# Expert weights in transfers of 4 MB with 32 KB runs, and the column order of W1 that goes with them

## What is computed

```python
for e in range(32):
    gu = tok @ w1[e] + b1[e]                       # w1[e]: 1024 x 2048
    gate = min(gu[:, :1024], 7); lin = clip(gu[:, 1024:], -7, 7)
    act = (lin + 1) * gate * sigmoid(1.702 * gate)
    out += combine[:, e:e+1] * (act @ w2[e] + b2[e])   # w2[e]: 1024 x 1024
```

## Time and profile before

| | |
|---|---|
| times of three executions | 1139.09, 1140.57, 1141.27 us |
| the profiled execution | 1139.39 us, its span 1137.7 us |
| PE busy | 1083.0 us (95%), 4926 matmul instructions |
| DVE, ACT busy | 195.9 us (17%), 139.7 us (12%) |
| DMA | 432.94 MB in 41954 packets, 381 GB/s over the span |
| large loads of expert weights | 191 of 2 MB, 42.1 us from issue to landing (median) |
| granted TensorE clock | 1.00 |

### The profile page before, as it was taken

The page is one execution under the profiler, slowest core; times in us unless marked ns, Lnnn a source line. Parts: engine busy times, 40 slices in busy tenths (PEclk is TensorE's granted clock), DMA queues, the critical chain, the costliest instruction groups (busy, mean ns, idle before and its releaser), DMA issues.

```text
span 1137.7 us, 11181 instructions
## 1 busy us (share of the span) xinstructions
PE 1083.0 (95%) x4926; PEld 423.5 (37%) x4926; DVE 195.9 (17%) x499; ACT 139.7 (12%) x285; POOL 14.9 (1%) x34
## 2 busy tenths in 40 slices
PE   7999999999999999999999989999999999999996
PEld 5474544733333333333333333333323333333332
DVE  1630011311211111111111111111111111111111
ACT  2114111201100001010000000000000000000001
POOL 0004000000000000000000000000000000000000
PEclk9999999999999999999999999999999999999999
DMA  9824526699999999999999999999999999999995
GB/s 346 322 105 148 220 75 262 273 424 429 427 429 425 429 427 428 427 428 429 426 429 427 428 427 429 427 427 428 427 428 429 427 428 427 429 426 429 427 428 217
DMA packets 41954, 432.94 MB, mean 381 GB/s; under 512 B 4252, under 2 KB 5808, under 8 KB 17328
## 3 DMA queue, kind: packets, MB, share of 16 engines
q1 hardware_dynamic: 40272, 431.26, 90.6%
q10 hardware_dynamic: 1632, 0.95, 0.3%
HBM read 431.14 MB, written 1.05 MB: 380 GB/s over the span
## 4 chain that ended last, share of the span: by engine, by line
PE 64%; DMA 35%; DVE 1%; ACT 0%; issue 0%; DVEq 0%; ACTq 0%
DMA ring<-in_expert_w_dram 34%; PE bank L314 23%; PE bank L329 11%; PE bank L956 9%; PE bank L338 4%; PE bank L1112 2%; PE bank L1092 2%; PE bank L304 2%; PE bank L275 2%; PE bank L320 1%; PE bank L1017 1%; PE bank L291 1%; PE bank L296 1%; PE bank L946 1%; PE bank L1039 0%; PE bank L284 0%
## 5 line engine op out<-in xcount | busy, mean ns | idle before, releaser
L314 PE MATMUL bank<-ring,work 128*64 128x512 f32 x2048 | 450.5, 595 | 19.0 <-DMA ring<-in_expert_w_dram 19.0
L314 PEld LDWEIGHTS bank<-ring,work 128*64 128x64 f32 x2048 | 142.3, 137 | 324.9 <-issue 280.2
L329 PE MATMUL bank<-ring,work 128*64 128x512 f32 x1024 | 229.5, 594 | 19.5 <-DMA ring<-in_expert_w_dram 19.0
L329 PEld LDWEIGHTS bank<-ring,work 128*64 128x64 f32 x1024 | 72.2, 137 | 170.9 <-issue 135.2
L870 DVE TENSOR_SCALAR work<-bank 128x512 f32<-128x512 f32 x32 | 22.1, 692 | 480.0 <-PE bank L314 480.0
L956 PE MATMUL bank<-ring 128*128 128x512 f32 x224 | 98.5, 594 | 0.0
L650 ACT ACTIVATE work<-work 128x512 f32<-128x512 f32 x32 | 20.2, 630 | 515.8 <-DVE work L870 515.8
L338 PE MATMUL bank<-work,putT 64*128 64x512 f32 x256 | 63.6, 615 | 0.8 <-ACT work L670 0.8
L360 DVE TENSOR_TENSOR work<-bank,vecs 128x512 f32<-128x512 f32 x32 | 22.1, 692 | 228.3 <-PE bank L291 227.2
L956 PEld LDWEIGHTS bank<-ring 128*128 128x128 f32 x224 | 41.8, 190 | 48.4 <-issue 48.2
L275 PE MATMUL bank<-xn,pick 128*64 128x512 f32 x248 | 58.6, 593 | 0.0
(11 more groups left out here) (179 smaller groups left out, 443.5 us busy)
## 6 DMA issues: line engine op xcount, KB each, us to landing
ring<-in_expert_w_dram SPq DMA_DIRECT2D x191, 2048.0 KB, 42.1
ring<-in_w_in_dram SPq DMA_DIRECT2D x8, 2048.0 KB, 19.7
ring<-in_w_out_dram SPq DMA_DIRECT2D x2, 2048.0 KB, 7.8
ring<-in_w_branch_attn_dram SPq DMA_DIRECT2D x1, 2048.0 KB, 8.2
ring<-in_w_branch_pool_dram SPq DMA_DIRECT2D x1, 2048.0 KB, 7.6
ring<-in_w_in_dram SPq DMA_DIRECT2D x1, 1296.0 KB, 7.8
xs<-in_x_dram SPq DMA_DIRECT2D x2, 512.0 KB, 4.2
ring<-in_expert_w_dram SPq DMA_DIRECT2D x1, 1024.0 KB, 42.8
```

The lines of the kernel that those rows point to most:

```text
L314: mm = pe.matmul(dst, hTe[:, at:at + SLOTS], w[:, col:col + BANK], start=(k == 0 and not bias_first), stop=(k == KD - 1 and bias_first), s ...
L329: mm = pe.matmul(ps_out[SLOTS * half:SLOTS * (half + 1), :], actT_e[:, at:at + SLOTS], w[:, col:col + BANK], start=(k == 0), stop=(k == KD ...
```

## The change

The ring becomes 5 places of 4 MB. An expert's W1 is two transfers and its W2 one, and a partition holds 4 rows of W1 or 8 of W2: one run of 32 KB. While blocks and scratch still share the ring, and for the refill of expert 2's W1, the seven first chunks (`IN_HALVES`) go in halves of 2 MB, each with a semaphore of its own, in the same order of waits as before; blocks lie in halves of three places. W2's last transfer goes in four pieces.

With 8 rows of W2 in a partition, hidden columns 8g to 8g+7 belong to partition g. PE gets that order by the way it reads W1: `quarter` takes four columns, skips four, and so on; quarter 0 is the first four of each eight, quarter 1 the others. The bias is read in the same way from rows twice as wide, of which both quarters hold a copy. `down` then uses the same transposes with step 4. Reading the gathered rows and the first picks, `every` has step 4 instead of 2; the router's transposes (L1118) and its weights are in plain order, for which a second copy of the gain (`V_GR`) is transposed: eight tiny transposes at L996 instead of two.

```diff
-    RING = 10
-    CHUNK_N = 4096
+    RING = 5
+    CHUNK_N = 8192
+    HALF_N = CHUNK_N // 2
-    SLOT_ORDER = (1, 9, 2, 3, 4, 6, 7, 8, 5, 0)
+    SLOT_ORDER = (0, 1, 3, 4, 2)
+    IN_HALVES = RING + W1_CHUNKS
...
-            base = S0 * CHUNK_N + slot * 2048 + at
+            base = S0 * HALF_N + (0, 1, 5, 6, 7, 2, 3, 4)[slot] * 2048 + at
...
-        TAIL = ((0, 2), (2, 3), (3, 4))
+        TAIL = ((0, 4), (4, 6), (6, 7), (7, 8))
...
-            return ring[:, i % POSITIONS, :]
+            at = (i - 1) % POSITIONS
+            return ring[:, at // 2, at % 2 * HALF_N:(at % 2 + 1) * HALF_N]
...
+        def quarter(ap, q):
+            at = q // 2 * FE
+            return ap[:, at:at + FE].rearrange("p (g h i) -> p h g i", h=2, i=4)[:, q % 2]
...
-                mm = pe.matmul(dst, bias_pick[rows, :], b1_rows[rows, :], start=first, stop=not first, skip_group_check=True)
+                mm = pe.matmul(dst, bias_pick[rows, :], quarter(b1_rows[rows, :], q % 2), start=first, stop=not first,
+                               skip_group_check=True)
...
-                    col = a * 2 * FE + q * BANK
-                    mm = pe.matmul(dst, hTe[:, at:at + SLOTS], w[:, col:col + BANK],
+                    mm = pe.matmul(dst, hTe[:, at:at + SLOTS], quarter(w[:, a * 2 * FE:(a + 1) * 2 * FE], q),
...
             used(B_G0 + 2)
-            load_w1(0, 0)
+            w1_half(0, 0, 0)
             sp.wait_ge(s["attn_ps"], TT)
-            load_w1(0, 1)
+            w1_half(1, 0, 1)
             used(B_G0 + 3)
-            load_w1(0, 2)
+            w1_half(0, 0, 1)
             used(B_WP)
-            load_w1(0, 3)
-            for c in (0, 1):
-                load_w1(1, c)
+            w1_half(0, 1, 0)
+            w1_half(0, 1, 1)
+            w1_half(1, 0, 0)
             sp.wait_ge(s["mergedT_ps"], 2 * TT)
-            for c in (2, 3):
-                load_w1(1, c)
+            w1_half(1, 1, 0)
+            w1_half(1, 1, 1)
             used(B_WO)
-            for c in range(W2_CHUNKS):
-                load_w2(0, c)
+            for h in range(2):
+                load_half(w2_chunk(0, 0), h, w2_dram(0, 0))
+            for c in range(W1_CHUNKS):
+                for h in range(2):
+                    if (c, h) != (W1_CHUNKS - 1, 1):
+                        sp.wait_ge(half_used, 2 * c + h + 1)
+                    else:
+                        sp.wait_ge(gemm1, 1)
+                    w1_half(2, c, h)
...
-                    sp.wait_ge(chunk_used, n + 1 - sum(last < n for last in W1_LAST + W2_LAST))
+                    sp.wait_ge(half_used, 3 * W1_FIRST.index(n) + 2)
 
             for e in range(1, E):
-                if e < E - 1:
+                if 1 < e < E - 1:
                     for c in range(W1_CHUNKS):
                         slot_free(w1_chunk(e + 1, c) - RING)
-                        load_w1(e + 1, c)
-                for c in range(W2_CHUNKS):
-                    slot_free(w2_chunk(e, c) - RING)
-                    if (e, c) != (E - 1, W2_CHUNKS - 1):
-                        load_w2(e, c)
-                        continue
-                    n, src = w2_chunk(e, c), w2_dram(e, c)
+                        load(w1_chunk(e + 1, c), w1_dram(e + 1, c))
+                n, src = w2_chunk(e, 0), w2_dram(e, 0)
+                slot_free(n - RING)
+                if e < E - 1:
+                    load(n, src)
+                else:
                     for i, (a, b) in enumerate(TAIL):
...
-                mm = pe.transpose(bank[4][:, at:at + W1_CHUNKS], every(g2_rows, W1_ROWS, a), ident[0:W1_CHUNKS, 0:W1_CHUNKS])
+                pe.transpose(bank[4][:, at:at + W1_CHUNKS], every(g2_rows, W1_ROWS, a), ident[0:W1_CHUNKS, 0:W1_CHUNKS])
+                at += KD
+                mm = pe.transpose(bank[4][:, at:at + W1_CHUNKS], g2_rows[:, a * P:(a + 1) * P], ident[0:W1_CHUNKS, 0:W1_CHUNKS])
...
-                    mm = pe.transpose(ps[:, j * P:(j + 1) * P], every(xs[:, tt, :], W1_ROWS, k), ident[:, :])
+                    mm = pe.transpose(ps[:, j * P:(j + 1) * P], xs[:, tt, k * P:(k + 1) * P], ident[:, :])
...
-                    pe.wait_ge(*chunk_landed(n))
-                    mm = up(pe, chunk_slot(n), c)
-                    if c < W1_CHUNKS - 1:
-                        mm.then_inc(chunk_used, 1)
+                    if n >= IN_HALVES:
+                        pe.wait_ge(*chunk_landed(n))
+                    for h in range(2):
+                        if n < IN_HALVES:
+                            pe.wait_ge(*half_landed(n, h))
+                        mm = up(pe, chunk_slot(n), c, range(2 * h, 2 * h + 2))
+                        if (c, h) != (W1_CHUNKS - 1, 1):
+                            mm.then_inc(half_used, 1)
                 mm.then_inc(gemm1, 1)
...
                 n = w2_chunk(E - 1, 0)
-                pe.wait_ge(*chunk_landed(n))
-                down(pe, chunk_slot(n), 0)
-                scatter(pe).then_inc(scattered, 1)
-                n = w2_chunk(E - 1, 1)
                 for i, (a, b) in enumerate(TAIL):
                     pe.wait_ge(tail_in[i], 16)
-                    mm = down(pe, chunk_slot(n), 1, range(a, b))
+                    mm = down(pe, chunk_slot(n), 0, range(a, b))
+                    if i == 0:
+                        scatter(pe).then_inc(scattered, 1)
```

More of the change, by code:

```diff
@@ L91, in scratch @@
         def scratch(slot, at, size):
-            flat = ring[:, :, :].rearrange("p s n -> p (s n)")
-            base = S0 * CHUNK_N + slot * 2048 + at
-            return flat[:, base:base + size]
+            base = S0 * HALF_N + (0, 1, 5, 6, 7, 2, 3, 4)[slot] * 2048 + at
+            return ring[:, :, :].rearrange("p s n -> p (s n)")[:, base:base + size]
         hT = scratch(0, 0, KD * T).rearrange("p (k t) -> p k t", k=KD)
@@ L142, in block_kernel @@
         vec_rows = putT[0:10, 0:P]
[L143 to L144 removed]
+        vecs = sb("vecs", [P, 34])
+        V_G1, V_PB, V_PS, V_QK, V_G2, V_GR = 0, 8, 12, 16, 18, 26
         pool_wsb = sb("pool_wsb", [P, G, P])
@@ L176, in block_kernel @@
         chunk_in = [sem(f"chunk_in{i}") for i in range(RING)]
-        TAIL = ((0, 2), (2, 3), (3, 4))
+        half_in = [[sem(f"half_in{i}_{h}") for h in range(2)] for i in range(RING)]
+        TAIL = ((0, 4), (4, 6), (6, 7), (7, 8))
         tail_in = [sem(f"tail_in{i}") for i in range(len(TAIL))]
-        chunk_used = sem("chunk_used")
+        half_used = sem("half_used")
         names = """gain_in consts inv_ok ident_ok vec_row_ok vec_ps vec_ok x_rms x_norm xT_ps hT_dve hT_act
@@ L244, in w2_chunk @@
             return (e + 1) * (W1_CHUNKS + W2_CHUNKS) + (W1_CHUNKS - W2_CHUNKS if e < E - 1 else -W2_CHUNKS) + c
+        W1_FIRST = [w1_chunk(e, 0) for e in range(E)]
         W1_LAST = [w1_chunk(e, W1_CHUNKS - 1) for e in range(E)]
@@ L252, in chunk_landed, with half_landed @@
         def chunk_landed(n):
-            return chunk_in[n % RING], 16 * (n // RING + 1)
+            return chunk_in[n % RING], 16 * (n // RING - (IN_HALVES - 1 - n % RING) // RING)
+        def half_landed(n, h):
+            return half_in[n % RING][h], 16 * (n // RING + 1)
         def w1_dram(e, c):
@@ L303, in up_bias, with up @@
                 rows = slice(E * q, E * (q + 1))
-                mm = pe.matmul(dst, bias_pick[rows, :], b1_rows[rows, :], start=first, stop=not first, skip_group_check=True)
-            return mm
-        def up(pe, w, c, bias_first=True):
-            for a in range(W1_ROWS):
+                mm = pe.matmul(dst, bias_pick[rows, :], quarter(b1_rows[rows, :], q % 2), start=first, stop=not first,
+                               skip_group_check=True)
+            return mm
+        def up(pe, w, c, rows=range(W1_ROWS), bias_first=True):
+            for a in rows:
                 k = c * W1_ROWS + a
@@ L319, in transpose_act @@
             for j in range(4):
-                mm = pe.transpose(ps_gate[:, j * P:(j + 1) * P], every(act_e, W2_ROWS, j), ident[:, :])
+                mm = pe.transpose(ps_gate[:, j * P:(j + 1) * P], every(act_e, 4, j), ident[:, :])
             return mm
@@ L395, in load_block, with load, load_half, w1_half @@
                 sp.dma_start(dst, src.rearrange("(k p) n -> p k n", p=P)).then_inc(block_in[i], 16)
[L397 to L403, removed]
+            def load(n, src):
+                sp.dma_start(chunk_slot(n), src).then_inc(chunk_in[n % RING], 16)
+            def load_half(n, h, src):
+                cols = slice(h * HALF_N, (h + 1) * HALF_N)
+                sp.dma_start(chunk_slot(n)[:, cols], src[:, cols]).then_inc(half_in[n % RING][h], 16)
+            def w1_half(e, c, h):
+                load_half(w1_chunk(e, c), h, w1_dram(e, c))
             for i in range(N_BLOCKS):
@@ L527, in _ @@
                               src.rearrange("a (h d) -> a h d", h=1).to_broadcast([1, 2, HD])).then_inc(s["vec_row_ok"], 16)
```

(15 more changed lines are left out.)

10 lines of the change are left out of this document (5 added, 5 removed).

## The result

The median after is 1150.01 us (six executions, 1148.12 to 1153.11) beside 1140.63 us for the kernel before (six, 1139.09 to 1141.27). The ratio is 1.0080, with an interval of [1.0067, 1.0094]: slower by 9.4 us, where 0.2 us less was forecast. The profiled execution took 1149.25 us, its span is 1147.5 us, 9.8 us above that of before. These 9.8 us are what has to be found.

What follows compares the result with a forecast made beforehand. The prediction took the DMA stream of expert weights, with its start and PE tail, as the bound. Terms -6.3 + 3.4 + 2.2 + 0.5 = -0.2 us gave 1140.4 us beside the median of 1140.57; range 1136.2 to 1147.0.

Steps and rivals of the forecast that it cites:

- PE before the stream: PE work ahead of the weight stream: more gain transposes, plain router transposes, step four in L284 free; together +0.5 us.
- The rule on lines of 16 bytes: SBUF accesses within one 16-byte line run at full rate, each new line costs something; L314's four-column read would be free.
- Longer runs: Expert weight DMA: 88 whole transfers with 32 KB runs take 0.73% less time, -6.3 us, bounds nothing to 8 us saved.
- the straight line through 2 KB and 16 KB: DMA run cost from two measured run sizes: 0.03687 ns a byte and 9.0 ns a run.
- half a semaphore write a run: DMA packets: half a semaphore write for each run, eight runs to a transfer, counted within the 9.0 ns a run.
- Both rivals with less saving: Expert weight DMA: no saving from 32 KB runs, 1146.7 us, chance 0.08; half the saving, 1143.6 us, chance 0.10.
- a lower DMA rate: Rival: 128 weight runs starting 32 KB apart slow DMA; 1155 us at one per cent, chance 0.05.
- The gap: DMA waits at the first whole transfer, expert 1's W2, near 248 us: +2.2 us, bounds 1.0 and 3.2.
- The tail: At the end, 32 instead of 16 L329 instructions stand after expert 30's W2 lands: +3.4 us.
- PE's reading of W1: L314's moving operand takes four columns, skips four: no cost, with 2.3 us of cover an expert.
- The rival with PE as the bound: L314 stretches by over a sixth, so PE sets the pace; at double some 1530 us, chance 0.05.
- The laggards lag less: Rival: slow DMA engines trail less in the tail, half of 7 us, 3.5 us: 1136.9 us, chance 0.13.

Runs made afterwards that it cites:

- the split transfers: The changed kernel with normed rows written in PE's reading order, each whole 4 MB transfer issued as two of 2 MB with 16 KB runs: 1147.89 us.
- the experiment: The kernel before with L314's moving operand reading every fourth column of W1: 1575.11 us.

## Why the prediction was wrong

*The step that failed* is one clause in "PE before the stream": "L284 takes every fourth element instead of every second; L320 (fourth) and L291 (second) load 209 ns each: nothing." The rows were read rightly and did not carry over. L320 and L291 are transposes, whose loads take 209 ns with either step, and do so after the change too: L303, the old L291, now with step four, 211 ns. L284's loads took 196 ns with step two and 329 with step four, and 16 of its instructions 3.73 us instead of 1.99. I priced the line from another kind of instruction, though the trace had L284 itself, whose 196 ns say nothing of step four. No row showed that case, and the forecast gave this edit one value and no bounds. The rule on lines of 16 bytes was quoted for the moving operand of L314 and not tried on L284, which with step four takes one f32 from each line.

*What it measured.* The late start of 9.65 us instead of 0.5 is 0.30 from before 211 us (forecast 0.5), 1.75 for the first 16 instructions (to the start of the next group 3.57 instead of 1.82), 1.85 for the second (3.79 instead of 1.94), and the rest, 5.75, for the half clock: all between them and the first half of expert 0's up. The step's own price is 3.6 us, somewhat over a third. The clock's is the larger part; without the step no profile has the 17.1 us, and why it falls is open, as said above. No rival had a change of clock in it: the earlier trace rows have 1.00 everywhere.

*Longer runs*, -6.3: the rates, the packets and the split transfers say 6.1, and the balance of the two profiles 2.71 + 3.3 = 6.0. Right; the straight line through 2 KB and 16 KB holds to 32 KB. Its bracket "half a semaphore write a run" does not come out of the rows: 2838 small packets beside 22,707 large ones are one for eight runs. The 6.1 us contain those of the 88 transfers saved as well. Both rivals with less saving fall, and so does a lower DMA rate. The Trainium skill ("DMA: Bandwidth & Descriptors", section "Why small descriptors are slow (HBM only)") has a smaller cost for a packet, from which I had an estimate of 2.5 us saved; the runs say 6.1.

*The gap*, +2.2 with bounds 1.0 and 3.2: 3.3 us. The place was right (DMA at 33 GB/s from 256 to 258 us, restart at 257.97), the size is just past the upper bound. I had priced one gap; as the kernel with expert 1's W2 in halves shows, the loss moves to the next whole transfers when that one is split. My reading, which no run tests, is that the queue is short there until PE waits for DMA.

*The tail*, +3.4: PE's part is 7.09 instead of 3.65 us, 3.4 us exactly; 0.5 us came back between the start of the last scatter and the end (6.8 us instead of 7.3), where the four transfers of the output landed in 2.6 us instead of 3.1, which no edit explains. Missed was the gap of 2.7 us ahead of it (1.16 before) in which the clock can fall: +1.5 to +1.7 us in four of the five profiles that have it.

*PE's reading of W1*, nothing: 596 ns and 13.88 us an expert. Right. The rival with PE as the bound had the right mechanism on the wrong access: with one column in four it is the 1575 us of the experiment (forecast 1530).

*The laggards lag less*: no. DMA's rate in the tail falls from about 1124.5 us and reaches nothing at about 1131.5, 7 us as before.

Without the failed clause the forecast's sum would have come to +0.45 us (0.3 - 2.71 + 2.86), and the kernel without it measured 1.0000. Its terms were off by up to 1.1 us, in opposite ways (gap 3.3 instead of 2.2, tail 2.9 instead of 3.4); that they nearly cancel is luck.

## What to carry to other kernels

Price a change of an operand's step from a row of the same kind of instruction (weights of a matmul, weights of a transpose, moving operand), and where there is none give it bounds, however few instructions it touches. For f32, count elements in 16 bytes: for a matmul's operands two or more were free here and one about doubled the time, while a transpose paid for step two as much as for step four. Where a path lengthens just ahead of the point that starts a stream, look at the granted clock there: here a stretch of small matmuls with slow loads, and in other places an idle gap of 2.3 to 2.8 us, went with a fall, and in the picks that cost more than the lengthening. Coarser transfers pay by their runs along the stream and cost at its end; keep the last one or two fine.

## What the runs showed of the hardware

Four things I had not expected. A weight load of 128x128 f32 takes 192, 196 and 329 ns in the picks' matmuls with plain columns, step two and step four, and 144, 209 and 211 ns in a transpose.

The clock level of 0.50 comes in spells of 3.4, 6.8 and 17.1 us: behind PE gaps of 2.3 to 2.8 us (not each time), and in or behind stretches of small matmuls in which PE was idle for 0.7 us at most. At 0.50 the 16 picks with slow loads take 3.99 us instead of 3.73, the bias behind them 1.98 instead of 1.09. The kernel before has spells too, though not in its profile: in 17 of its 49 executions beside the experiments its mean granted clock is 0.994 to 0.997, and these took 1142.2 to 1145.0 us; the 32 at 0.999 or 1.000 took 1138.6 to 1141.7.

When the clock rises to 1.00 at the start of the span varies from 10.0 to 16.6 us between profiles. With the latest rise the picks began at 213.41 us, in the profile of the kernel before at 210.94, and nothing ahead of them had been edited: 2.5 us.

And 32 KB runs that start 32 KB apart lose nothing on 16 engines. From 388, 428 and 431 GB/s at 2, 16 and 32 KB the cost of a run is, by estimate, some 9 ns over the whole width.
